# Token combinations moved into the stages ahead, three double blocks multiplied by seven products, one factor moved to VectorE

## The reference, cut to what matters

```python
def first_block(x, ...):
    h = h + 0.5 * swiglu_ffn(rmsnorm(h, norm_ffn1), ffn1_w_in, ffn1_w_out)      # FFN 0
    u = rmsnorm(h, norm_mix); ...                                              # pooling and retention mixer
    h = h + merged @ w_out                                                     # output projection 1
    h = h + 0.5 * swiglu_ffn(rmsnorm(h, norm_ffn2), ffn2_w_in, ffn2_w_out)      # FFN 1
    return rmsnorm(h, norm_final)

def second_block(x, ...):
    h = x
    h = h + 0.5 * swiglu_ffn_2(rmsnorm_2(h, ffn1_norm), ffn1_w_in, ffn1_w_out)  # FFN 2
    ...                                                                        # convolution and gated delta rule
    h = h + concatenate([y_conv, y_gdn]) @ w_mix_out                           # output projection 2
    h = h + 0.5 * swiglu_ffn_2(rmsnorm_2(h, ffn2_norm), ffn2_w_in, ffn2_w_out)  # FFN 3
    return rmsnorm_2(h, final_norm)

def swiglu_ffn(x, w_in, w_out):
    gate, up = jnp.split(x @ w_in, 2, axis=-1)
    return (jax.nn.silu(gate) * up) @ w_out
```

## Time and profile before

| | us |
|---|---|
| median of 3 runs | 2166.02 (2165.83 to 2166.07) |
| profiled execution | 2165.71 |
| its span, first to last instruction | 2163.9 |
| TensorE busy | 2142.9 (99% of the span) |
| VectorE busy | 1540.6 (71%) |
| ScalarE busy | 885.0 (41%) |
| GpSimd busy | 214.7 (10%) |
| mean granted TensorE clock | 0.997 |

### The profile page before, as it was taken

One profiled execution on the slowest core, in us unless ns is written; L12 is line 12 of the kernel. 1 busy time (PEld: TensorE's weight loads), 2 busy tenths in 40 slices (PEclk: granted clock), 3 DMA queues, 4 the chain that ended last, 5 costly groups with the idle time before them and its releaser, 6 DMA issues.

```text
span 2163.9 us, 30238 instructions
## 1 busy us (share of the span) xinstructions
PE 2142.9 (99%) x12568; PEld 1897.1 (88%) x12568; DVE 1540.6 (71%) x1743; ACT 885.0 (41%) x1104; POOL 214.7 (10%) x167
## 2 busy tenths in 40 slices
PE   8999999999999999999999999999999999999998
PEld 7998998888777888998998798999788888998997
DVE  8975976453466547884896996697788768874983
ACT  6432543232233425441444443244572256442443
POOL 0000003610123001000003300000102002000002
PEclk9999999999999999999999999999999999999999
DMA  4332332232222223242332123233221123232331
GB/s 161 108 127 72 105 116 97 98 117 98 78 80 76 88 97 127 78 137 69 107 128 97 62 95 129 76 106 109 88 66 63 58 78 117 97 129 75 101 129 47
DMA packets 59175, 210.37 MB, mean 97 GB/s; under 512 B 6560, under 2 KB 8992, under 8 KB 58784
## 3 DMA queue, kind: packets, MB, share of 16 engines
q1 hardware_dynamic: 58464, 205.30, 28.3%
q0 software_dynamic: 288, 2.62, 0.3%
q10 hardware_dynamic: 288, 0.52, 0.1%
HBM read 206.33 MB, written 2.10 MB: 96 GB/s over the span
## 4 chain that ended last, share of the span: by engine, by line
PE 96%; DVE 2%; issue 1%; DMA 0%; POOL 0%; ACT 0%; POOLq 0%; SPq 0%; DVEq 0%
PE accs L667 27%; PE accs L669 27%; PE accs L668 27%; PE mixbs L668 3%; PE mixbs L667 3%; PE mixbs L669 3%; PE mixbs L1204 1%; PE mixbs L1227 1%; PE accs L1166 1%; PE accs L1164 1%; PE accs L1165 1%; DVE w_lo L1795 0%; PE mixbs L1049 0%; PE accs L1060 0%; PE mixbs L1060 0%
## 5 line engine op out<-in xcount | busy, mean ns | idle before, releaser
L1288 ACT ACTIVATE w_hi<-w_raw 128x1024 fp32r<-128x1024 f32 x491 | 509.2, 1054 | 587.2 <-PE accs L669 280.3
L1795 DVE TENSOR_TENSOR w_lo<-w_raw,w_hi 128x1024 fp32r<-128x1024 f32 x491 | 613.1, 1252 | 105.5 <-ACT w_hi L1288 99.1
L667 PE MATMUL accs<-x_hi,w_hi 128*128 128x512 f32 (+1 forms) x1440 | 507.7, 353 | 8.1 <-DVE x_lo L1837 7.4
L669 PE MATMUL accs<-x_hi,w_lo 128*128 128x512 f32 (+1 forms) x1440 | 501.0, 348 | 0.0
L668 PE MATMUL accs<-x_lo,w_hi 128*128 128x512 f32 (+1 forms) x1440 | 500.7, 348 | 0.0
L667 PEld LDWEIGHTS accs<-x_hi,w_hi 128*128 128x128 f32 x1440 | 273.6, 190 | 42.5 <-DVE x_lo L1837 8.1
L669 PEld LDWEIGHTS accs<-x_hi,w_lo 128*128 128x128 f32 x1440 | 273.3, 190 | 34.6
L668 PEld LDWEIGHTS accs<-x_lo,w_hi 128*128 128x128 f32 x1440 | 273.7, 190 | 32.8
L667 PE MATMUL accs<-hid_hi,w_hi 128*128 128x512 f32 (+1 forms) x714 | 275.9, 386 | 0.0
L668 PE MATMUL accs<-hid_lo,w_hi 128*128 128x512 f32 (+1 forms) x714 | 275.9, 386 | 0.0
L669 PE MATMUL accs<-hid_hi,w_lo 128*128 128x512 f32 (+1 forms) x714 | 275.8, 386 | 0.0
(11 more groups left out here) (404 smaller groups left out, 3065.6 us busy)
## 6 DMA issues: line engine op xcount, KB each, us to landing
w_raw<-weights SPq DMA_DIRECT2D x383, 512.0 KB, 3.2
y_t<-h SPq DMA_DIRECT2D x16, 128.0 KB, 1.9
h<-x_t SPq DMA_DIRECT2D x3, 512.0 KB, 6.4
k1c<-const POOLq DMA_DIRECT2D x1, 1536.0 KB, 7.4
k2c<-const POOLq DMA_DIRECT2D x1, 1024.0 KB, 8.0
h<-x_t ACTq DMA_DIRECT2D x2, 256.0 KB, 4.1
w_raw<-weights SPq DMA_DIRECT2D x1, 384.0 KB, 4.8
cst<-const SPq DMA_DIRECT2D x1, 161.0 KB, 7.9
```

The source lines that it names most:

```text
L667: pe.matmul(bank, w_hi[:, n % HI_SLOTS, w], hi, start=start, stop=False, skip_group_check=read_between)
L669: return pe.matmul(bank, w_lo[LO[n]][:, w], hi, start=False, stop=stop, skip_group_check=read_between)
L1288: act.activation(w_hi[:, n % HI_SLOTS, :], w_raw[RAW[n]][:, :], ACT.Copy).then_inc(hi_split, 1)
L1795: dve.tensor_tensor(w_lo[LO[n]][:, :], w_raw[RAW[n]][:, :], w_hi[:, n % HI_SLOTS, :].bitcast(F32), ALU.subtract).then_inc(lo_split, 1)
```

## The change

`NPLAIN` becomes (2, 1, 1, 1): in FFN 1, 2 and 3 the second double is made of seven products. The time for the combinations is then one plain double; so `PRE` names pairs whose combination is made in the stage ahead: pairs 0 to 2 of FFN 1 (in `mix_out`) and of FFN 2 (in `ffn1_out1`), pairs 0 and 1 of FFN 3 (in `mix2_out`). `early_mix` on VectorE follows each tile's `x_lo`, and on odd tiles makes the rest of the pair before and mixes the present one; `early_round` on ScalarE rounds pair m/2 - 1 on even tiles. The other pairs stay in the plain double, whose order changes: in FFN 2 the first root is taken sooner (`chained_mean`, `chained_sum`), the sums of the norm stand one step later in their blocks, and the second one inside block 2. GpSimd's multiplication of h by `r_one` goes; VectorE makes the product of h, the gain and `r_one` in `add_tile` of `ffn2_out0`, and inverts `r_one` there.

```diff
--- before.py
+++ after.py
@@ -48,7 +48,9 @@
-NPLAIN = (2, 2, 2, 2)
+NPLAIN = (2, 1, 1, 1)
+
+PRE = ((), (0, 1, 2), (0, 1, 2), (0, 1))
 PHASES = [("ffn0_in0", 42 - 3 * NPLAIN[0]), ("ffn0_out0", 12), ("ffn0_in1", 35), ("ffn0_out1", 10), ("pool_in", 4), ("v", 4), ("pool_in2", 4),
@@ -786,11 +788,16 @@
                 dense(n + 1, a + 1, x_hi, x_lo, middle=(lambda: split_sum(f"norm{r}")) if f else None,
-                      at={1: 2, 2: 0, 3: 4}.get(f, 0))
-                if f == 2:
-                    pe.wait_ge(h_chain, 1)
-                    split_sum("norm3b", square2_r)
-                dense(n + 2, a + 2, x_hi, x_lo, middle=None if f else lambda: split_sum("norm0"))
+                      at={1: 2, 2: 1, 3: 4}.get(f, 0))
+
+                def second_sum():
+                    if f == 0:
+                        split_sum("norm0")
+                    if f == 2:
+                        pe.wait_ge(h_chain, 1)
+                        split_sum("norm3b", square2_r)
+
+                dense(n + 2, a + 2, x_hi, x_lo, middle=second_sum, at=0 if f else 3)
                 dense(n + 3, a + 3, x_hi, x_lo)
             def out_tiles(f, p):
@@ -1305,6 +1312,11 @@
+            def early_round(f, m):
+
+                if m and m % 2 == 0 and m // 2 - 1 in PRE[f]:
+                    round_mixed(f, m // 2 - 1)
+
             def residual(r, m, ready):
@@ -1378,11 +1390,15 @@
                     split(n0 + 2)
+                if f == 2:
+                    take_root("norm3", 1.0 / D, r_one[:, :])
                 split(n0 + 3)
+                late = [j for j in range(KD // 2) if j not in PRE[f]]
                 if f:
-                    round_mixed(f, 0)
+                    round_mixed(f, late[0])
                 split(n0 + 4)
-                take_root(f"norm{r}", 1.0 / D, r_one[:, :] if f == 2 else rstd[:, :])
+                if f != 2:
+                    take_root(f"norm{r}", 1.0 / D, rstd[:, :])
                 if f == 2:
@@ -1391,22 +1407,25 @@
                 silu_plain(d, 0)
-                round_mixed(f, 1 if f else 0)
+                if f == 0:
+                    round_mixed(f, 0)
+                elif late[1:]:
+                    round_mixed(f, late[1])
                 act.wait_ge(drained, a + 3)
...
                 split(n0 + 5)
-                round_mixed(f, 2 if f else 1)
+                if f == 0:
+                    round_mixed(f, 1)
             def plain_next(f, d, n0, a):
...
                 round_hidden(d - 1)
-                round_mixed(f, 3 if f else 2)
+                round_mixed(f, 2)
                 act.wait_ge(drained, a + 1)
...
                 split(n0 + 3)
-                if f == 0:
-                    round_mixed(f, 3)
+                round_mixed(f, 3)
                 split(n0 + 4)
@@ -1450,6 +1469,8 @@
                                         residual(after, m, (h_added, 16 * f + 8 + m + 1))
+                                        if after == 3:
+                                            early_round(2, m)
             def round_hidden(d):
@@ -1560,6 +1581,7 @@
                 residual(2, m, (drained, a + m + 1))
+                early_round(1, m)
             act.activation(w_ab[:, :, 0:8], vcol("w_ab", 0, 64).rearrange("p (k n) -> p k n", k=KD),
@@ -1747,6 +1769,7 @@
                     mixed_square(m - 1)
+                early_round(3, m)
                 if m % 2 == 0 and m < KD - 2:
@@ -1831,6 +1854,13 @@
+            def early_mix(f, m):
+
+                if m % 2 and (m - 3) // 2 in PRE[f]:
+                    mixed_rest(f, (m - 3) // 2)
+                if m % 2 and m // 2 in PRE[f]:
+                    mix_tokens(f, m // 2)
+
             def rest_of(r, m):
@@ -1841,17 +1871,16 @@
                 end, value = tile_end(f, p, m)
+                if f == 2 and p == 0:
+                    dve.scalar_tensor_tensor(h[:, m, :], h[:, m, :], vcol("norm_final", m), r_one[:, :], ALU.mult,
+                                             ALU.mult).then_inc(h_final, 1)
                 dve.wait_ge(END[end], value)
...
                                          ALU.mult).then_inc(drained, 1)
-                if f == 2 and p == 0 and m == 0:
-                    dve.wait_ge(h_final, KD)
+                if f == 2 and p == 0:
+                    dve.wait_ge(h_final, m + 1)
                 dve.wait_ge(drained, out0 + m + 1)
-                if f == 2 and p == 0:
-                    dve.scalar_tensor_tensor(h[:, m, :], h[:, m, :], vcol("norm_final", m), f_tmp[:, m % 2, :], ALU.mult,
-                                             ALU.add).then_inc(h_added, 1)
-                else:
-                    dve.tensor_tensor(h[:, m, :], h[:, m, :], f_tmp[:, m % 2, :], ALU.add).then_inc(h_added, 1)
+                dve.tensor_tensor(h[:, m, :], h[:, m, :], f_tmp[:, m % 2, :], ALU.add).then_inc(h_added, 1)
             def rest_sum(name, whole, pair=None):
@@ -1934,65 +1963,73 @@
-            def chained_roots():
+            def chained_mean():
...
                 dve.tensor_scalar(rstd[:, :], sums[:, :], EPS / D, EPS * EPS, ALU.mult, ALU.add).then_inc(h_chain, 1)
+
+            def chained_sum():
+
                 dve.wait_ge(summed, SUM["norm3b"] + 1)
...
                 dve.scalar_tensor_tensor(rstd[:, :], sums[:, :], 1.0 / D, rstd[:, :], ALU.mult, ALU.add).then_inc(h_chain, 1)
-                invert_root("norm3b", rstd[:, :])
             def plain_first(f, d, n0, a):
                 r = FFN_NORM[f]
+                late = [j for j in range(KD // 2) if j not in PRE[f]]
                 if f:
-                    mix_tokens(f, 0)
+                    mix_tokens(f, late[0])
                 rest_norm(r)
...
                     prepare(n0 + 2)
+                if f == 2:
+                    chained_mean()
                 prepare(n0 + 3)
-                if f:
-                    mix_tokens(f, 1)
-                prepare(n0 + 4)
+                if f and late[1:]:
+                    mix_tokens(f, late[1])
                 if f == 2:
-                    chained_roots()
-                else:
-                    invert_root(f"norm{r}", rstd[:, :])
+                    chained_sum()
+                before(n0 + 4)
+                if f != 2:
+                    split(n0 + 4)
+                invert_root("norm3b" if f == 2 else f"norm{r}", rstd[:, :])
                 gate_plain(d, n0, a, 0)
+                if f == 2:
+                    split(n0 + 4)
                 up_plain(d, n0 + 1, a, 0)
                 if f:
-                    mixed_rest(f, 0)
+                    mixed_rest(f, late[0])
                 else:
...
                 gate_plain(d, n0 + 2, a, 1)
-                mix_tokens(f, 2 if f else 1)
+                if f == 0:
+                    mix_tokens(f, 1)
                 prepare(n0 + 5)
-                mixed_rest(f, 1 if f else 0)
+                if f == 0:
+                    mixed_rest(f, 0)
+                elif late[1:]:
+                    mixed_rest(f, late[1])
                 up_plain(d, n0 + 3, a, 1)
             def plain_next(f, d, n0, a):
                 prepare(n0 + 2)
-                mix_tokens(f, 3 if f else 2)
+                mix_tokens(f, 2)
                 gate_plain(d, n0, a, 0)
...
                 prepare(n0 + 3)
-                mixed_rest(f, 2 if f else 1)
-                if f == 0:
-                    mix_tokens(f, 3)
+                mixed_rest(f, 1)
+                mix_tokens(f, 3)
                 up_plain(d, n0 + 1, a, 0)
-                if f == 2:
-                    invert_root("norm3", r_one[:, :])
                 prepare(n0 + 4)
                 gate_plain(d, n0 + 2, a, 1)
-                mixed_rest(f, 3 if f else 2)
+                mixed_rest(f, 2)
                 prepare(n0 + 5)
                 up_plain(d, n0 + 3, a, 1)
-                if f == 0:
-                    mixed_rest(f, 3)
+                mixed_rest(f, 3)
             def ffn(f):
@@ -2050,6 +2087,8 @@
                             hidden_rest(d)
+                            if f == 2 and p == 0:
+                                invert_root("norm3", r_one[:, :])
                         for m in range(KD):
@@ -2059,6 +2098,8 @@
                                 rest_of(after, m)
+                                if after == 3:
+                                    early_mix(2, m)
             def gated_mix(phase, sig0):
@@ -2233,6 +2274,7 @@
                 rest_of(2, m)
+                early_mix(1, m)
             dve.wait_ge(rounded, 2)
@@ -2584,9 +2626,11 @@
                     rest_of(5, m - 1)
+                    early_mix(3, m - 1)
                 if m % 2 == 0 and m < KD - 2:
...
             rest_of(5, KD - 1)
+            early_mix(3, KD - 1)
             prepare(n + 3 + LEAD)
@@ -2614,12 +2658,6 @@
             def ffn(f):
-                if f == 2:
-
-                    pool.wait_ge(normed, WIDE["norm3"] + 1)
-                    pool.wait_ge(x_mixed, 12 * f + 12)
-                    for m in range(KD):
```

(1 more changed line is left out.)

## The result

The changed kernel takes 2186.8 us (2184.8 to 2188.1), the kernel before beside it 2166.1: a ratio of 1.0094 [1.008, 1.0108]. The forecast was 2180 us with a range up to 2187, so the sign and two of three stages came out as worked; the time lies 6.8 us over the forecast, 0.2 us inside the upper end of the range, and two of the four runs (2187.1 and 2188.1) lie past it. The profiled execution took 2186.5 us, its span is 2184.7, 20.8 more than before. The page's chain of waits, by engine, answers to the earlier trace rows: TensorE has lost four points, VectorE and ScalarE have taken them.

The account below looks back on a forecast made before the run. TensorE was taken to bound the kernel (96% of the span). Net border terms 5.0 + 0.5 + 8.2 plus 0.7 for the clock gave +14.4 us on 2165.71, so 2180 us, range 2170 to 2187.

Parts of the forecast that it names:

- What bounds the kernel: Whole kernel: TensorE is 96% of the span; VectorE's apparent free time is 1.31 us holes before x_lo, unusable in program order.
- stage C: Output projection 2 into FFN 3: block 0's weights late, block 1 8.0 us late, second product waits 1.8; net +8.2 us.
- What is taken away: Three plain doubles save 1.60 us each; FFN 2's input phase loses 7.56 us of waiting, 5.0 at its first seven-product double.
- Stage A: Output projection 1 into FFN 1: block 1 starts 5.6 us late, norm's sum waits 1.0, less 1.6; net +5.0 us.
- Stage B: FFN 1's second output phase into FFN 2: block 1 7.2 us late, sum waits 2.5, less 7.56 and 1.6; net +0.5.
- R3: Low clock behind the three borders' waits not covered, 1.5 us each, and output projection 2's border at 9.1: 2185 us; chance 0.10.
- R2: In the three stages ahead only VectorE's own work counts; roundings and GpSimd cost nothing: 2171 us; chance 0.13.
- R4: Borders at output projections 1 and 2 half as late as walked: about 2165 to 2168 us, no difference; chance 0.05.
- R1: Combinations fall into VectorE's idle time in the three stages, last x_lo keeps its time, gain arrives: 2154.1 us; chance 0.10.

Follow-up runs that it names:

- gap-placed FFN 1: Factor-alone kernel plus FFN 1 changed, its mixes and rests put in VectorE's gap before x_lo, ScalarE's rounding before the square: 2159.6 us.
- experiment 4: Meant here: FFN 1 and FFN 2 both changed with pieces in VectorE's gaps, FFN 2's norm sums first, against the original kernel: 2160.3 us, 0.9972.
- experiment 3: Two variants of the kernel with FFN 3 alone changed (2173.7 us): GpSimd copies norm5's squares instead of summing, 2169.0; ScalarE rounds behind the weight split, 2168.5.

## Why the prediction was right, and where it was not

*What bounds the kernel* was right: but for 0.6 us at the program's start, what the change costs is TensorE's waits at the three borders and the stretches at half clock behind them, and VectorE's idle share of before was no measure of what fits in. That the time fell inside the range is in part luck: the upper end of 2187 was drawn around 2185, a clock never covered and stage C at 9.1, and what took the time there was stage C at 13.7.

*What is taken away.* FFN 2's input phase with the factor moved lost 5.04 us, for the 5.0 read from the block starts. The product on VectorE cost nothing, as forecast. "The weight loads stay the same in number" holds for the transfers of weights (383 of 512 KB in both kernels) but not for TensorE's own, which rise from 12568 to 12784; no time is seen for them. The 1.60 us a double are seen clean in the gap-placed FFN 1 (124.66 to 123.06).

*Stage A* came out as walked: block 1 starts 5.7 us late (5.6), the sum waits 0.8 (1.0), together +5.0 (+5.0). With the clock at half behind the same waits, in the trace with FFN 1 alone, FFN 1's phase was 0.7 us dearer, so most of that stretch is covered there, as the forecast had it.

*Stage B*: TensorE waits 7.1 us before block 1 (7.2) and starts it 8.2 late, since the last step of block 0 already runs at half clock. Block 1 takes 7.95 us where 5.90 would do (5.44 and two sum matmuls), 2.05 more (2.5 forecast, as a wait for the sum alone): 0.8 of it is waiting, the rest the low clock. That the low clock would fall into time in which the sum wasn't there anyway was forecast, and is so but for at most the 0.7 us by which the border is dearer than +0.5.

*Stage C* is the term that was mis-sized: +13.7 for +8.2. The mechanism (mix, rounding, split and rest in the same turn, weights of block 0 late) was right. The step that failed is the price of GpSimd's overlap, "a doubling of up to three operations, 2.2 us more" as the worst for the way to the weights of block 0. The count was right: three operations met a sum before those weights, one in the first mix and both in the first rest. What was wrong is that an operation doubles: each got 1.0 to 1.1 us longer whatever its own length, 3.2 us together, so that the one of 0.40 us more than trebled. The weights came 27.2 us after the stage's start, where 23.8 had been walked and 26.0 was the worst (1808.0 and 1810.2 less 1784.2). Two more such meetings, 2.15 us, fell on the rest of pair 1. Block 1 starts 10.9 late (8.0, bound 9.1; by its own terms, 1810.2 + 7.4 + 2.1 + 1.15 less 1811.6, the bound comes to 9.25). The second product waited 2.9 (1.8), and the clock behind it, where nothing more is late, took 1.55. 2.9 (10.9 less 8.0) + 1.1 + 1.55 are the 5.5 us that the border is dearer. The last two are not fixed: in the trace with FFN 3 alone the stretch at half clock fell elsewhere, the second product waited 1.3 us, and the border cost 12.2 us.

The Trainium skill, "SBUF — State Buffer", section "Who interferes with whom", calls the port pair of VectorE and GpSimd an exclusive lock. The rows of border C agree in that an operation of VectorE that meets a sum grows by a time that doesn't follow its own length (0.40 to 1.43, 0.87 to 1.98 from start to start). They don't agree with blocking for the whole of the other's instruction, as the prediction put it: the operation of 1809.62 begins 0.07 us behind a sum of 1.64 us and grows by 1.11. The prediction's reading of that rule, 9.1, was still too low, since it doubled short operations instead of adding a time to each.

*The rivals.* R3's 2185 is nearer the measured time than the forecast, and part of its mechanism is there: once (the second product of FFN 3) the low clock was not covered, and it was not covered in experiment 4 either. At A the clock didn't fall in the changed kernel's trace, and did with FFN 1 alone. R2 is excluded by experiment 3: the rounding's place and GpSimd's sums are each worth some 5 us at border C. R4 is excluded by the borders: A cost +5.0 and C +13.7, neither half of what was walked. R1 is right on another placing: what it supposed, that the combinations fall into VectorE's idle time, is what the gap placing does in FFN 1.

## What to carry to other kernels

Idle time on an in-order engine is a place, not a budget: look at what ends each gap, and put the added work in front of that wait. The same operations in output projection 1 cost 7.5 us behind x_lo (5.9 and the 1.6 saved) and nothing ahead of it, with the rounding moved too. Where a helper engine slows the one on the path, count the meetings and add the same time for each, however short the operation (here up to 1.1 us beside a sum and 0.4 beside a copy). And before trading a new wait of TensorE against a saving of 1.6 us, price a stretch at half clock behind it: where it came and nothing else was late it cost 1.5 to 1.9 us here, though it didn't come behind every wait.

## What the runs showed of the hardware

A wait of TensorE and the clock behind it: 5.5 us of waiting at B and at C were followed by 6.8 us at 1.2 GHz counted from inside the wait, 2.9 us (second product of FFN 3) and 2.6 (experiment 4) by about 3.4 us. At A waits of 1.5 and 3.5 us, 8 us apart, were followed by no such stretch in the changed kernel, where the granted clock of that window is 1.00, and by 3.4 us of it in the kernel with FFN 1 alone. With the late rounding, waits of 2.3 and 1.8 us, 3 us apart, were followed by none. So the length of one wait alone does not say whether the clock falls: the same two waits did both. What does isn't settled by these runs.

The meeting of the two engines is one-sided. GpSimd's sum of 128 by 512 elements takes 1.55 and 1.64 us in the rows of border C and 1.29 in FFN 1's input phase of the kernel before, where VectorE's x_lo came 0.6 us behind its start:

```profile
841.79 1.29 POOL L2606 TENSOR_TENSOR sumsq<-sumsq,square 128x512 f32<-128x512 f32 x1 [4.14 <-ACT square L1295]
```

VectorE's operation of 0.40 us takes 1.43 beside such a sum: GpSimd loses 0.3 where VectorE loses 1.0. A copy of GpSimd, 0.66 to 0.80 us, costs VectorE's operations 0.4 each.
